# Modulation weights in four column blocks on the quadrants of partitions, and another place for their background jobs

## The reference, cut to what matters

```python
c_act = jax.nn.silu(c)                            # c: (1, 1024)
mod = c_act @ w_ada[l] + b_ada[l]                 # w_ada: (1024, 6*1024)
sh1, sc1, g1, sh2, sc2, g2 = split(mod, 6)
h = _rmsnorm(x, norm_attn_g[l]) * (1.0 + sc1) + sh1
...
# second block, for each of 2 layers and for two conditions, c_2 and c_ctx_2:
mod = silu(c) @ w_ada_2[l] + b_ada_2[l]           # w_ada_2: (1024, 9*1024)
a, b = jnp.split(modulate(rms_norm(h, g), shift, scale) @ w13, 2)     # D_FF 2816
h = h + 0.5 * gate * ((silu(a) * b) @ w2)
```

## Time and profile before

| | us |
|---|---|
| median of 3 runs | 3689.54 |
| lowest, highest | 3684.26, 3697.37 |
| span of the profiled execution, first to last instruction | 3679.9 |
| PE busy in the span | 3511.9 |
| DVE busy | 2154.9 |
| ACT busy | 1032.2 |

### The profile page before, as it was taken

The page is one execution under the profiler, slowest core; times in us unless marked ns, Lnnn a source line. Parts: engine busy times, 40 slices in busy tenths (PEclk is TensorE's granted clock), DMA queues, the critical chain, the costliest instruction groups (busy, mean ns, idle before and its releaser), DMA issues. The chain is left out here.

```text
span 3679.9 us, 49835 instructions
## 1 busy us (share of the span) xinstructions
PE 3511.9 (95%) x20487; PEld 2893.2 (79%) x20487; DVE 2154.9 (59%) x5075; ACT 1032.2 (28%) x1604; POOL 133.0 (4%) x116
## 2 busy tenths in 40 slices
PE   7998989999999999899999999989999999999998
PEld 5755868887888888774688888878888887578887
DVE  7555566557666565854455657575656636543334
ACT  3454023223321212333432121222121124432222
POOL 0012010000000000100000000010000010000000
PEclk9998889999999999998999999999999999999999
DMA  6532034443324342420123434333333323023331
GB/s 181 148 87 61 3 98 118 123 119 111 89 84 115 93 120 82 118 68 12 32 67 91 117 91 115 93 97 86 104 102 97 107 56 101 20 69 98 92 102 64
DMA packets 637196, 333.92 MB, mean 91 GB/s; under 512 B 21891, under 2 KB 633191, under 8 KB 636712
## 3 DMA queue, kind: packets, MB, share of 16 engines
q1 hardware_dynamic: 636612, 330.60, 31.9%
q10 hardware_dynamic: 356, 0.14, 0.0%
HBM read 328.57 MB, written 2.77 MB: 90 GB/s over the span
## 5 line engine op out<-in xcount | busy, mean ns | idle before, releaser
L2078 PE MATMUL psum<-hn_high,high 128*128 128x512 f32 (+1 forms) x3136 | 1128.3, 360 | 8.4 <-DVE low L2522 8.4
L2080 PE MATMUL psum<-hn_high,low 128*128 128x512 f32 (+1 forms) x3136 | 1111.9, 355 | 0.0
L2079 PE MATMUL psum<-hn_low,high 128*128 128x512 f32 (+1 forms) x3136 | 1108.5, 353 | 0.0
L2078 PEld LDWEIGHTS psum<-hn_high,high 128*128 128x128 f32 x3136 | 593.4, 189 | 110.6 <-issue 16.7
L2080 PEld LDWEIGHTS psum<-hn_high,low 128*128 128x128 f32 x3136 | 591.5, 189 | 87.5
L2079 PEld LDWEIGHTS psum<-hn_low,high 128*128 128x128 f32 x3136 | 592.6, 189 | 84.7 <-issue 0.5
L2605 DVE SCALAR_TENSOR_TENSOR partial<-stage,cond,partial 128x128 f32<-128x128 f32 x2304 | 622.8, 345 | 0.0
L2522 DVE TENSOR_TENSOR low<-stage,high 128x1024 fp32r<-128x1024 f32 (+2 forms) x415 | 493.4, 1209 | 179.4 <-ACT high L1759 178.9
L1759 ACT ACTIVATE high<-stage 128x1024 fp32r<-128x1024 f32 (+2 forms) x415 | 415.3, 1025 | 516.2 <-DMA stage<-in_w_ffn 373.3
L2078 PE MATMUL psum<-hidden_high,high 128*128 128x512 f32 (+1 forms) x1408 | 500.7, 356 | 1.6 <-DVE hidden_low L2527 1.5
L2080 PE MATMUL psum<-hidden_high,low 128*128 128x512 f32 (+1 forms) x1408 | 494.5, 351 | 0.0
(11 more groups left out here) (314 smaller groups left out, 3167.5 us busy)
## 6 DMA issues: line engine op xcount, KB each, us to landing
stage<-in_w_ffn SPq DMA_DIRECT2D x240, 512.0 KB, 4.3
stage<-in_w_ada SPq DMA_DIRECT2D x192, 512.0 KB, 4.0
stage<-in_w_in SPq DMA_DIRECT2D x48, 512.0 KB, 5.3
stage<-in_w_out SPq DMA_DIRECT2D x24, 512.0 KB, 4.2
stage<-in_w_ffn SPq DMA_DIRECT2D x32, 384.0 KB, 4.2
stage<-in_w_gate SPq DMA_DIRECT2D x22, 512.0 KB, 3.9
stage<-in_w_up SPq DMA_DIRECT2D x22, 512.0 KB, 5.1
stage<-in_w_down SPq DMA_DIRECT2D x16, 512.0 KB, 4.1
```

The source lines that it names most:

```text
L2078: self.e.matmul(out, high[:, i], xh, start=first and n == 0, stop=False)
L2079: self.e.matmul(out, high[:, i], xl, start=False, stop=False)
L2080: done = self.e.matmul(out, low[:, i], xh, start=False, stop=last and n == nk - 1)
```

## The change

A modulation load takes 256 of the 1024 rows of four neighbouring column blocks in place of all rows of one. Rows are given to partitions so that partition p of each group of 32 (a quadrant) holds rows 32p to 32p+31, and the job's part (0 to 3) selects eight of these; column block q lies on quadrant q. The load is four DMAs of 128 KB, each to 32 partitions. Four jobs (a quad) add into the same sums, and only after the fourth do PE and DVE finish them: two matmuls against a 128x4 matrix of ones on the quadrants (`quarter`) and one addition of the bias for four column blocks. The conditions are loaded in the same layout, one DMA for each quadrant, straight to `cond_rows`, and SP waits for the first sigmoid before it loads the other two.

In SwiGLUs with two parts the job of each down tile is gone, and each gate and up tile (but the first) has a second job, behind the context part's matmuls and ahead of its `gated_tile`.

```diff
@@ -171,7 +172,8 @@
         self.vec = sb("vec", [P, 3, P])
         self.mod1 = sb("mod1", [P, N_MOD1 * KT, 1])
         self.mod2 = [sb(f"mod2_{n}", [P, N_MOD2 * KT, 2]) for n in range(2)]
-        self.cond = sb("cond", [P, KT, 3])
+        self.cond = sb("cond", [P, 3, QROWS])
+        self.quarter = sb("quarter", [P, 4])
         self.gain = sb("gain", [P, KT, 3])
         self.small = sb("small", [P, 144])
         self.partial = sb("partial", [P, 2, 2, P])
...
@@ -480,7 +480,10 @@
         stage = self.stages.next()
         raw = stage.ap[:, 0:nk * cols]
         dst, at, moves = raw.rearrange("p (k n) -> p k n", k=nk), 0, []
-        for c, width in (c0 if isinstance(c0, tuple) else ((c0, cols),)):
+        if isinstance(k0, tuple):
+            rows = w.rearrange("(p r) n -> p r n", r=QROWS)[:, k0[0]:k0[0] + nk]
+            moves = [(dst[32 * q:32 * q + 32], rows[:, :, c0 + q * P:c0 + (q + 1) * P]) for q in range(4)]
+        for c, width in () if moves else (c0 if isinstance(c0, tuple) else ((c0, cols),)):
             moves.append((dst[:, :, at:at + width], w[k0:k0 + nk * P, c:c + width].rearrange("(k p) n -> p k n", p=P)))
             at += width
         self.load_block(n, stage, moves)
...
@@ -685,13 +688,18 @@
 
 
     def modulation(self, w, layer, j, mod, vectors, bias):
-        name = layer, j
-        n, stage, view = self.weights(w, 0, KT, j * P, split=False)
-        part = self.partials.next()
-        self.modulation_sums(name, n, view, part, vectors)
+
+        quad, part = j // 4, j % 4
+        name = layer, quad, part
+        n, stage, view = self.weights(w, (part * KT,), KT, quad * 4 * P, split=False)
+        if part == 0:
+            self.sums = self.partials.next()
+        self.modulation_sums(name, n, view, self.sums, vectors, part)
         stage.free = [("mod_sums", name)]
         self.finish_modulation()
-        self.unfinished = name, part, mod[:, j, :], len(vectors), bias[:, j:j + 1]
+        if part == 3:
+            at = slice(4 * quad, 4 * quad + 4)
+            self.unfinished = name, self.sums, mod[:, at, :], len(vectors), bias[:, at]
 
     def finish_modulation(self):
         if self.unfinished:
...
@@ -727,8 +735,8 @@
         self.load_first()
         if self.board.plan is not None:
             self.load_to(STAGES - 1)
+        self.take_condition(0)
         self.take_vectors(0, 1)
-        self.take_condition(0, "c")
         self.load_start()
 
     def take_vectors(self, lo, hi):
...
@@ -736,9 +744,9 @@
         self.turn_vectors(bank, lo, hi)
         bank.free = [("vec", lo)]
 
-    def take_condition(self, n, name):
+    def take_condition(self, n):
         t = self.temps.next()
-        self.condition(n, self.mem.column(name, KT), t, ("vec", 0 if n == 0 else 1))
+        self.condition(n, self.mem.cond_rows[:, n, :], t)
         t.free = [("cond", n)]
 
     def token_tile(self, k):
...
@@ -1191,6 +1199,8 @@
                         self.products(("up_sum", key), bank_b.ap[:, 0:T], n_b, wb, part.hn, 0, [])
                     if n == len(parts) - 1:
                         self.pump()
+                        if n and at:
+                            self.pump_background()
                     t = self.temps.next()
                     high, low = hidden[n]
                     self.gated_tile(key, bank_a.ap[:, 0:T], bank_b.ap[:, 0:T], t, t.ap[:, 0:T], high[:, f, :], low[:, f, :],
...
@@ -1200,8 +1210,6 @@
                 slot_a.free = slot_b.free = [last]
             for f in range(KT):
                 n_d, slot, view = self.weights(w_down, first * P, tiles, f * P)
-                if len(parts) > 1:
-                    self.pump_background()
                 for n, part in enumerate(parts):
                     bank = self.banks.next()
                     key = name, first, f, n
...
@@ -1608,14 +1616,25 @@
 
 
     def load_first(self):
+        self.load_condition(0, self.mem.inp["c"][0])
         self.dma(self.misc(), ("eye",), self.mem.eye[:], self.mem.const["eye"])
         self.wait_ge("cleared")
         for n, (tile, dst, src) in enumerate(self.mem.rows):
             if tile == 0:
                 self.dma(self.misc(), ("row", n), dst, src)
 
+    def load_condition(self, n, c):
+        rows = c.rearrange("(p r) -> p r", r=QROWS)
+        for q in range(4):
+            self.dma_counts["cond_landed"] = self.dma_counts.get("cond_landed", 0) + 16
+            self.e.dma_start(self.mem.cond_rows[32 * q:32 * q + 32, n, :], rows).then_inc(self.sems["cond_landed"], 16)
+        self.board.new["cond_rows", n] = "cond_landed", self.dma_counts["cond_landed"]
+
     def load_start(self):
         mem, i = self.mem, self.mem.inp
+        self.wait_ge("cond_sigmoid", 0)
+        self.load_condition(1, i["c_2"][0])
+        self.load_condition(2, i["c_ctx_2"])
         col = lambda ap: ap.rearrange("(n o) -> n o", o=1)
         self.dma(self.misc(), ("tokens", "main"), mem.tokens_main, i["x"][0].rearrange("(a p) n -> p a n", p=P))
         self.dma(self.misc(), ("small", 0), mem.dt_bias, col(i["dt_bias"][0]))
...
@@ -2136,10 +2157,11 @@
     def modulation_vector(self, name, part, bank, n, mod, bias):
         both = n == 2
         self.wait_ge("mod_sums", name)
+        self.wait_ge("quarter")
         self.wait_free(bank)
         for i in range(2):
-            at = i if both else 0
-            done = self.e.matmul(bank.ap[:, at:at + 1], part.ap[:, i, :], self.mem.ones[:, 0:1], start=both or i == 0,
+            at = 4 * i if both else 0
+            done = self.e.matmul(bank.ap[:, at:at + 4], part.ap[:, i, :], self.mem.quarter[:, :], start=both or i == 0,
                                  stop=both or i == 1)
         done.then_inc(*self.mark("mod_psum", name))
 
...
@@ -2585,20 +2607,22 @@
         self.e.scalar_tensor_tensor(x, x, self.mem.column(name, 1, skip=k), rinv, ALU.mult, ALU.mult) \
             .then_inc(*self.mark("scaled", name, k))
 
-    def modulation_sums(self, name, n, view, part, vectors):
+    def modulation_sums(self, name, n, view, part, vectors, quarter):
 
         both = len(vectors) == 2
         self.wait_ge("landed", n)
         for c in vectors:
             self.wait_ge("cond", c)
-        self.wait_free(part)
-        at = [0, 0]
+        if quarter == 0:
+            self.wait_free(part)
+            self.sums_at = [0, 0]
+        at = self.sums_at
         for k in range(KT):
             for i, c in enumerate(vectors):
                 x = i if both else k % 2
-                acc, by = part.ap[:, x, :], self.mem.cond[:, k, c:c + 1]
+                acc, by = part.ap[:, x, :], self.mem.cond[:, c, quarter * KT + k:quarter * KT + k + 1]
                 inc = self.mark("mod_sums", name) if k == KT - 1 and i == len(vectors) - 1 else self.step()
-                if k < (1 if both else 2):
+                if not at[x]:
                     self.e.tensor_scalar(acc, view[:, k, :], by, None, ALU.mult).then_inc(*inc)
                 else:
                     self.wait_own(at[x])
...
@@ -2607,11 +2631,18 @@
 
     def modulation_vector(self, name, part, bank, n, mod, bias):
         self.wait_ge("mod_psum", name)
-        self.e.tensor_scalar(mod, bank.ap[:, 0:n], bias, None, ALU.add).then_inc(*self.mark("mod", name))
+        self.e.tensor_tensor(mod, bank.ap[:, 0:4 * n].rearrange("p (v q) -> p q v", v=n),
+                             bias.rearrange("p (q o) -> p q o", o=1).broadcast_to([P, 4, n]), ALU.add) \
+            .then_inc(*self.mark("mod", name))
 
     def clear(self):
         self.e.memset(self.mem.vectors, 0.0).then_inc(*self.mark("cleared"))
         self.e.memset(self.mem.ones[:], 1.0).then_inc(*self.mark("ones"))
+        self.e.memset(self.mem.quarter[:], 0.0).then_inc(*self.step())
+        self.wait_own()
+        for q in range(4):
+            inc = self.mark("quarter") if q == 3 else self.step()
+            self.e.memset(self.mem.quarter[32 * q:32 * q + 32, q:q + 1], 1.0).then_inc(*inc)
 
     def turn_vectors(self, bank, lo, hi):
         self.wait_ge("vec_turned", lo)
...
```

More of the change, by code:

```diff
@@ L45 @@
 MISC = 24
+QROWS = D // 32
 COMPUTE = ("tensor_wrote", "scalar_wrote", "vector_wrote", "pool_wrote")
@@ L229, in start_maps @@
         put("b_ada", 0, 24, rows_of(i["b_ada"][0]))
-        put("c", 0, 72, rows_of(i["c"][0]))
-        put("conv", 0, 80, i["conv_w"][0].rearrange("j (r p) -> (j r) p", p=P))
+        put("conv", 0, 72, i["conv_w"][0].rearrange("j (r p) -> (j r) p", p=P))
         for l in range(2):
@@ L242, in start_maps @@
             put(f"g_qb{l}", t, 102, i["g_q_2"][l, P:Q_RANK].rearrange("(r p) -> r p", p=Q_RANK - P))
-        put("c2", 1, 103, rows_of(i["c_2"][0]))
-        put("c_ctx", 1, 111, rows_of(i["c_ctx_2"]))
-        put("final2", 1, 119, rows_of(i["g_final_2"]))
+        put("final2", 1, 103, rows_of(i["g_final_2"]))
         self.tokens_main = self.area("tokens", 4 * D).rearrange("p (a n) -> p a n", a=4)
```

(19 more changed lines are left out.)

## The result

| | before | after |
|---|---|---|
| median of 4 runs, us | 3686.90 | 3804.01 |
| lowest, highest | 3681.83, 3697.37 | 3803.20, 3804.80 |
| span of the profiled execution | 3679.9 | 3802.3 |

A forecast was written before the change was run, and what follows sets the result against it. It took PE, busy 3511.9 of 3679.9 us, to be the bound. The terms -17 - 52 + 13 + 107 + 3 gave +54 us on the span, 3734, and 3743 as the median (+1.5%), range 3672 to 3815.

The forecast's parts named there:

- step 1: First block: three of four modulation vectors go, 38 at 0.45 us of PE time each, a gain of 17 us.
- step 4: Gate and up tiles with two jobs: a loop through DMA buffers lengthens tiles from 17.1 to 19.7 us, 107 us lost.
- L: Time from the end of job B's sums until the next wa load has landed: 6.1 us, from 5.0 to 7.9.
- X: Shortest gate and up tile under the loop, L + 13.6 = 19.7 us, where before it took 17.1.
- Step 2: Shared down tiles without jobs: 30 us of vectors and 22 us of waits go, a gain of 52 us (41 to 56).
- Step 3: Three jobs forced at once on DVE ahead of `ffn2`, layer 0, with PE idle: 13 us lost (12 to 16).
- Step 5: Program start: earlier DVE and fewer bias additions against later tokens; 3 us lost (4 less to 8 more).
- slow quadrants: Rival: loads to a quadrant run at two thirds of the rate, 3.0 us for 512 KB, L 7.1, 3786 us; chance 0.05.
- slow landing: Rival: issues back up in the loop, L 7.2 to 7.9, X 20.8 to 21.5, 3790 to 3820 us; chance 0.09.
- The loop doesn't hold: Rival: two-job tiles take 0.22 us less than before, 3622 us; chance 0.15 together with X under 18.4.

The follow-up runs named there:

- experiment 5: Changed kernel with the jobs in their old places and 704 unused bytes a partition behind `cond`: 3649.29 us against 3687.47 for the kernel before (0.9898).
- experiment 4: Kernel before with only the places of the jobs changed; loads, sums and vectors stay old: 3760.79 us (1.0207 of the kernel before).
- experiment 2: Changed kernel with 704 unused bytes a partition more, so later tiles stand 1024 bytes from where they stood: 3778.12 us (1.0254 of the kernel before).
- experiment 3: Changed kernel with the jobs in their old places, quadrant loads and four-job sums kept: 3692.10 us (1.0019 of the kernel before).
- experiment 8: Changed kernel with a tile's second job directly behind the first, ahead of main's gated tile: 3798.34 us (1.0304 of the kernel before).
- experiment 9: Changed kernel with the second job directly behind the first and a quad's vector emitted one job later: 3672.89 us against 3688.74 before (0.9956).
- experiment 11: Changed kernel, jobs in old places, 704 unused bytes, and the second block's two conditions loaded behind the fourth job: 3651.59 us (0.9896 of the kernel before).
- experiment 6: Changed kernel with each column block on every fourth partition in place of a quadrant: 3857.14 us (1.0463 of the kernel before).
- experiment 7: Changed kernel with a load's four pieces issued for quadrants 0, 2, 1, 3: 3804.24 us (1.0306 of the kernel before).
- experiment 1: Kernel before with only 320 unused bytes a partition behind `cond`: 3715.43 us against 3685.41 (1.0083).
- experiment 10: Changed kernel, second job directly behind the first, a quad's vector one job later, 704 unused bytes: 3632.86 us (0.9845 of the kernel before).

## Why the prediction was right in sign and short in size

The span grew 68 us more than the +54 of the sum. Three terms failed: step 1 (a gain of 17 us that didn't come), the landing in step 4's loop (6.8 us in place of 6.1 for L), and the start (9.4 us in place of 3); and the cost of the tiles' placement stood in no step. That 3804 lies inside 3672 to 3815 all the same is in part luck: the range was made from values of X, and X was only 0.5 us off.

**Step 1 (fewer vectors in the first block, -17): failed, +3.5.** Part is the pace, which no step had. With the pace restored (experiment 5) the SwiGLU's 14 tiles between first and last of its groups of 8 gain 4.8 us, as 10.5 vectors of 0.45 should; the linear layers and the output layer gain nothing, 2 us are lost (experiment 4, the same kernel as before up to there, differs by 3 us, so that this is no more than none). PE waits there for other things (gates, `hn`, projections): its idle time in this stretch grows by 7 us (45 to 52), and the vectors saved went into that. I had priced them as if PE were the bound in all of the block.

**Step 2 (down tiles, -52, up to -56, with +10 at the groups' ends): more, -71,** though part of that is DVE's lag coming back, and the placement took 15 us out of it (experiment 2 against the change).

**Step 3 (forced jobs, +13): right,** 12.85.

**Step 4 (the loop): the mechanism was right, the term L was sized short.** The issues took 1.9 us as said; the landing took 5.0, not 4.2, so L = 6.8 in place of 6.1. X - L was 13.4 (said 13.6), X = 20.2 in place of 19.7, 43 x 0.5 = 21 us of the 35 that the shared half steps are off. I had taken the landing of a load "with little ahead of it"; wa goes out right behind the four pieces, and the row for two in a row (5.4) was the nearer one. Experiments 3, 8 and 9 show that the loop and the vector's place make the loss: away from both, tiles take 17.1 us. The placement covers about the rest: it costs 16 us in these stretches, 1 in the gate and up tiles and 15 in the down tiles and between (experiment 2 against the change).

Step 4 also said "What vectors are left in these tiles cost nothing". Where quads end on B, PE waits up to 4.8 us at the head of each second tile, 31.5 us in ten times in `ffn2`, layer 0, and works at the lower clock behind it. Yet the gate and up tiles of that half step lost 57 us, and those of `ffn1`, layer 0, which have none of these waits but 31.6 us of waits for splits, lost 54. This wait thus stands in the place of the loop's, and about 3 us of it come on top. The later vector with job B in the change's own place wasn't tried.

**Step 5 (start, +3): short, +9.4.** DVE's first sums began 2.1 us later and not earlier (9.41 against 7.36), and the tokens went out at 16.7, not 14; by the fifth block's sums 7.3 us were lost (experiment 11), against which the gains I had counted, 2 us and 2.4, are small. The loads were also slower than my reading of the earlier trace rows had it: one load last in a queue, at 261 GB/s, says little about sixteen blocks. The trace has 227 for quadrants and 286 for whole columns, 2.3 and 1.8 us for a block of 512 KB; four pieces on every fourth partition ran at 297 (experiment 6), so it is the quadrant and not the piece that is slow. The ports' rule (the Trainium skill, "SBUF — State Buffer", the section on the DMA port swizzle) has partitions 0 to 31 on 8 of 16 ports; by the 435 GB/s that the Trainium skill gives for all, an estimate for half is 218, and the trace agrees with its 227. The rival "slow quadrants" had the mechanism, with 3.0 us a block too dear, and was wrong about where it counts: I had charged it to the loop, and there pieces in another order changed nothing (experiment 7) and spread ones made it worse by their issue (experiment 6).

**Not in any step: the placement,** 26 to 30 us (experiments 1 and 2), about two fifths of the 68. It lies where PE is the bound: 4.5 us in `ffn2` of layer 1 alone, next to none in the gate and up tiles of the changed kernel. Where nothing else holds PE it costs more, 43 us (experiment 3 to 5) and 40 (9 to 10).

Of the rivals, "slow landing" (X from 20.8) was nearest in time, but by luck: no issues backed up in the loop, X was 20.2, and what brought the time there were costs that it didn't have. "The loop doesn't hold" is what experiment 10 built, 3633 against the 3622 worked out for it.

## What to carry to other kernels

When a kernel has a fixed ring of buffers, one more request per iteration ties each kind of load to its own buffer of the iteration before; write down the loop (release, issues ahead, landing, consumers in their order) and take the landing from a row with the same queue ahead. Put the consumer of such a ring as early in the iteration as it can go, and what reads its result a full iteration later; with groups of several jobs look at every phase in which a group can end. After any change of a tile's size compare the pace of a stretch in which nothing was changed: if that moved, suspect the addresses, and separate them from the change by padding.

## What the hardware showed that I had not expected

- 320 bytes a partition of shift slow matmuls of 512 columns from one in 228.4 ns to one in 232.0, over the whole program +0.8%; 1024 bytes of shift, the only other one tried, don't.
- Loads to one quadrant after another move 227 GB/s, whole columns 286; in the order 0, 2, 1, 3 it is 246, and on every fourth partition 297.
- A piece of 32 partitions costs SP 0.45 us of issue if the partitions are neighbours and 0.62 if every fourth is meant (1.81 and 2.50 for four pieces of a condition).
- Behind a wait of 3.56 us on PE the granted clock was 0.50 for 6.5 us, with matmuls 0.43 us apart; in the 14 us with the wait of 12.85 it was 0.76.

```profile
1916.00:1930.00 14.00, 10.38 (x64) 9.79 (x64) 12.39 (x31) 6.36 (x12) 0.00 (x0) 0.76 0.59 131
```
